# Gate/up weights of a top-2-of-8 expert layer in wider blocks, a gather in two steps, and expert rows turned in banks of their own

## The reference

```python
for i in range(2):
    z = rms_norm(h) @ w_in[i]                      # 1024 x 7168
    ... short convolutions, a gated linear recurrence, three 1024 x 1024 projections, residual add
    n2 = rms_norm(h)
    h += swiglu(n2, ffn_w_gu, ffn_w_dn)            # layer 0, width 3072
    h += moe_swiglu(n2, router, moe_w_gu, moe_w_dn)  # layer 1
    h += sigmoid(rms_norm(h) @ w_ple_gate[i]) * (p[i] @ w_ple_proj[i])

def moe_swiglu(x, router, w_gu, w_dn):   # top 2 of 8, softmax over the two logits
    for e in range(8):                   # w_gu[e] 1024 x 3072 (gate | up), w_dn[e] 1536 x 1024
        g, u = split(x @ w_gu[e])
        out += comb[:, e] * ((silu(g) * u) @ w_dn[e])
```

## Time and profile before

| | |
|---|---|
| profiled execution | 1185.72 us, span 1184.0 us |
| TensorE matmuls busy | 1126.7 us, 95% of the span |
| TensorE weight loads busy | 996.1 us, 84% |
| VectorE busy | 948.7 us, 80% |
| ScalarE busy | 721.0 us, 61% |
| moved by DMA | 289.55 MB, mean 245 GB/s |
| of it instructions, queue q8 | 92 packets, 1.51 MB |
| mean granted TensorE clock | 0.986 of full speed |
| costliest group | L1367 on VectorE, 179 of 2287 ns on the raw buffers |
| gate/up matmuls L879, L881, L882 | 1536 each, starts some 0.04 us apart |

### The profile page before, as it was taken

How to read it: one execution, slowest core, us unless ns; L and a number is a source line. 1 busy time by engine, 2 the same in 40 slices (tenths; PEclk the granted TensorE clock), 3 DMA queues, 4 the chain that set the end, 5 groups by cost and what they waited for, 6 DMA issues and landing times.

```text
span 1184.0 us, 31432 instructions
## 1 busy us (share of the span) xinstructions
PE 1126.7 (95%) x13839; PEld 996.1 (84%) x13839; DVE 948.7 (80%) x1011; ACT 721.0 (61%) x716; POOL 24.9 (2%) x59
## 2 busy tenths in 40 slices
PE   7999999999999999899999998899989998989997
PEld 4888888878888888688888885788989988988976
DVE  5986896786666657996788678499899899899877
ACT  4555744446555445445574436687888787688653
POOL 4000001000000001000000100000000000000000
PEclk7999999999999999999999999899999999999999
DMA  9665566645656563456565665699999999999911
GB/s 268 219 211 182 178 213 196 200 143 183 202 184 210 182 212 125 142 167 213 191 205 190 205 201 195 233 367 390 394 392 393 392 393 393 380 393 393 366 50 37
DMA packets 195672, 289.55 MB, mean 245 GB/s; under 512 B 5208, under 2 KB 132200, under 8 KB 195543
## 3 DMA queue, kind: packets, MB, share of 16 engines
q1 hardware_dynamic: 193830, 283.71, 68.8%
q0 software_dynamic: 1728, 4.16, 1.3%
HBM read 286.53 MB, written 1.52 MB: 243 GB/s over the span
## 4 chain that ended last, share of the span: by engine, by line
PE 78%; DVE 16%; ACT 3%; issue 2%; DMA 0%; SPq 0%; DVEq 0%; ACTq 0%
PE acc L600 16%; PE acc L602 16%; PE acc L601 16%; DVE wl L1367 10%; PE acc L879 4%; PE acc L881 3%; PE acc L882 3%; PE acc L914 2%; PE acc L585 2%; PE acc L592 2%; PE acc L586 2%; PE acc L931 2%; PE acc L934 2%; PE acc L933 2%; PE aux L832 2%
## 5 line engine op out<-in xcount | busy, mean ns | idle before, releaser
L1367 DVE SCALAR_TENSOR_TENSOR wl<-raw,wh 128x2048 f16<-128x2048 f32 x179 | 408.6, 2287 | 116.1 <-ACT wh L1012 115.4
L600 PE MATMUL acc<-xn,wh 128*128 128x264 f16 x1424 | 393.0, 276 | 0.6 <-DVE wl L1367 0.6
L602 PE MATMUL acc<-xn,wl 128*128 128x264 f16 x1424 | 393.0, 276 | 0.0
L601 PE MATMUL acc<-xn,wh 128*128 128x264 f16 x1424 | 393.0, 276 | 0.0
L1012 ACT ACTIVATE wh<-raw 128x2048 f16<-128x2048 f32 x179 | 340.2, 1907 | 7.7 <-PE acc L934 3.2
L879 PE MATMUL acc<-ga,wh 128*128 128x96 f16 x1536 | 204.3, 207 | 8.2 <-issue 4.7
L881 PE MATMUL acc<-ga,wh 128*128 128x96 f16 x1536 | 204.0, 207 | 3.9 <-issue 3.8
L882 PE MATMUL acc<-ga,wl 128*128 128x96 f16 x1536 | 204.0, 207 | 3.7 <-issue 3.7
L879 PEld LDWEIGHTS acc<-ga,wh 128*128 128x128 f16 x1536 | 151.3, 98 | 12.1 <-issue 11.5
L600 PEld LDWEIGHTS acc<-xn,wh 128*128 128x128 f16 x1424 | 139.3, 98 | 21.9 <-ACT wh L1012 0.8
L601 PEld LDWEIGHTS acc<-xn,wh 128*128 128x128 f16 x1424 | 139.3, 98 | 21.0
(11 more groups left out here) (304 smaller groups left out, 1861.7 us busy)
## 6 DMA issues: line engine op xcount, KB each, us to landing
raw<-in_w_in SPq DMA_DIRECT2D x56, 1024.0 KB, 5.1
raw<-in_moe_w_gu SPq DMA_DIRECT2D x38, 1024.0 KB, 13.0
raw<-in_ffn_w_gu SPq DMA_DIRECT2D x24, 1024.0 KB, 5.2
raw<-in_moe_w_dn SPq DMA_DIRECT2D x22, 1024.0 KB, 15.1
raw<-in_ffn_w_dn SPq DMA_DIRECT2D x12, 1024.0 KB, 5.1
ya<-in_moe_w_gu SPq DMA_DIRECT2D x11, 1024.0 KB, 14.1
xn<-in_moe_w_gu SPq DMA_DIRECT2D x11, 1024.0 KB, 13.8
xb<-in_moe_w_gu SPq DMA_DIRECT2D x10, 1024.0 KB, 14.4
```

What stands on the lines that cost most here:

```text
L600: nc.tensor.matmul(bank, hi, x[:, 0, x0 + k, :], start=(k == 0), stop=False)
L601: nc.tensor.matmul(bank, hi, x[:, 1, x0 + k, :], start=False, stop=False)
L602: last = nc.tensor.matmul(bank, lo, x[:, 0, x0 + k, :], start=False, stop=(k == k_chunks - 1))
L1367: op(V.scalar_tensor_tensor(out=wl[:, s, 0:size], in0=raw_slot[raw_turn(n)[0]][:, 0:size], scalar=WS, in1=wh[:, s, 0:size], op0=ALU.mult, ...
```

## The change

Gate/up units become 2 chunks by 1024 columns. Four units make a block of 1024 columns: gate columns 0 to 1023, then gate 1024 to 1535 with up 0 to 511, then up 512 to 1535. Both acc banks 0 and 1 are filled by one block and evacuated together after its fourth unit. Each step has two gate/up units. The gather of the next expert is done in two halves, after steps 0 and 1. The transposes of an expert's rows go to aux banks 2 and 3 (acc 0 and 1 for the last expert), and all experts keep acc banks 2 and 3 for the down projection.

```diff
-GU_K, DN_K = C // 2, 2
+GU_K, DN_K = 2, 2
+BLOCK = C // GU_K
 def gate_up_units(t):
-    return range(0 if t == 0 else 2 * t + 1, min(2 * t + 3, MOE_GU))
+    return range(2 * t, 2 * t + 2)
 # SP
-                            k, col = u % 2 * GU_K, u // 2 % 2 * FE + u // 4 * 512
-                            moe_load(gu_unit(i, u), gu[:, i, k:k + GU_K, col:col + 512], GU_K)
+                            k, col = u % BLOCK * GU_K, u // BLOCK * 1024
+                            moe_load(gu_unit(i, u), gu[:, i, k:k + GU_K, col:col + 1024], GU_K)
 # TensorE
+        def rows_bank(e, half):
+            return acc[0:CAP, half, :] if e == NE - 1 else aux[0:CAP, 2 + half, :]
-            def gather(e):
-                for g in range(4):
+            def gather(e, groups):
+                for g in groups:
...
+                    if e > 2 and g > 1:
+                        pe.wait_ge(ys_ready, 2 * (e - 3) + g - 1)
 # gate_or_up
+                for m in range(C):
+                    bank = acc[:, m // 4, m % 4 * CAP:(m % 4 + 1) * CAP]
+                    if s == 0 and m % 4 == 0:
+                        if block == 0 and e:
+                            pe.wait_ge(up_out, GROUPS * (e - 1) + m // 4 + 2)
+                        elif block == 1:
+                            pe.wait_ge(gate_out, GROUPS * e + m // 4 + 1)
+                        elif block == 2:
+                            pe.wait_ge(*((gate_out, GROUPS * e + 3) if m == 0 else (up_out, GROUPS * e + 1)))
             def slots_to_rows(e):
+                if e < NE - 1:
+                    pe.wait_ge(gat_done, 4 * min(e + 2, NE - 1) + 4)
+                    if e:
+                        pe.wait_ge(sc_done, 8 * e)
 # down
-                if d == 0 and e == NE - 1:
-                    pe.wait_ge(gate_out, GROUPS * NE)
-                    pe.wait_ge(up_out, GROUPS * NE)
-                elif d == 0 and e:
-                    pe.wait_ge(ys_ready, 2 * e)
+                if d == 0 and e:
+                    pe.wait_ge(down_out, 2 * e)
 # TensorE's loop
                     if i + 1 < NE and t == 0:
                         pe.wait_ge(sel_ready, i + 2)
-                        gather(i + 1)
+                        gather(i + 1, (0, 1))
                     if i + 1 < NE and t == 1:
+                        gather(i + 1, (2, 3))
                         selected_slots(i + 1)
 # ScalarE, after the router's Exp
+            nc.scalar.activation(root[:], eps[:], ACT.Silu)
 # ScalarE, gate_or_up
-                if u % 4 == 1 and q:
+                if u == 1 and e:
+                    hidden_hi(q - 2)
                     hidden_hi(q - 1)
+                if u == 9:
+                    hidden_hi(q)
+                if u % BLOCK == BLOCK - 1:
+                    act.wait_ge(unit_mm, n + 1)
+                    if u == BLOCK - 1:
+                        if e:
+                            act.wait_ge(hid_w, q)
+                        gate(0)
+                        gate(1)
+                    elif u == 2 * BLOCK - 1:
+                        gate(2)
+                        up(0)
+                    else:
+                        up(1)
+                        act.wait_ge(hid_w, q + 1)
+                        up(2)
 # ScalarE and VectorE, the loops
-                            if i > 1 and u == 0:
+                            if i > 1 and u == 1:
                                 expert_out(i - 2)
 # VectorE, gate_or_up
+                if u == 2 * BLOCK - 1:
+                    product(0)
+                if u == MOE_GU - 1:
+                    product(1)
+                    product(2)
-                    if i + 1 < NE and t == 2:
+                    if i + 1 < NE and t == 3:
                         slot_weights(i + 1)
```

More of the change, by code:

```diff
@@ L119, in gu_unit @@
 def gu_unit(e, u):
-    return moe_base(e) + u + (max(u - 1, 0) // 2 if e else 0)
+    return moe_base(e) + u + (u // 2 if e else 0)
 def dn_unit(e, d):
@@ L852, in scatter @@
                         pe.wait_ge(selt_ready, min(e + 4, NE))
-                    pe.wait_ge(ys_ready, 2 * e + c // 4 + 1)
+                    pe.wait_ge(ys_ready, 2 * e + (2 if c > 2 else 1))
                     if c < 4 and e + 3 >= NE and e:
@@ L861, in gate_or_up @@
             def gate_or_up(e, u):
[L863 to L868, removed]
+                n, s, block = gu_unit(e, u), u % BLOCK, u // BLOCK
+                if block == 0:
+                    pe.wait_ge(gat_done, 4 * e + s + 1)
                 pe.wait_ge(hi_done, TURN[n] + 1)
@@ L877, in gate_or_up @@
                         x_hi, x_lo = (xg[:, e % 2, i, s * GU_K + k, :] for i in range(2))
-                        end = s == 1 and k == GU_K - 1
-                        nc.tensor.matmul(bank, hi, x_hi, start=(s == 0 and m == 0 and k == 0), stop=False,
+                        end = s == BLOCK - 1 and k == GU_K - 1
+                        nc.tensor.matmul(bank, hi, x_hi, start=(s == 0 and m % 4 == 0 and k == 0), stop=False,
                                          skip_group_check=True)
@@ L893, in slots_to_rows @@
                         at = (4 * half + m) * CAP
-                        last = nc.tensor.transpose(acc[0:CAP, ye_bank(e) + half, m * P:(m + 1) * P], yt[:, at:at + CAP],
+                        last = nc.tensor.transpose(rows_bank(e, half)[:, m * P:(m + 1) * P], yt[:, at:at + CAP],
                                                    ident[:])
@@ L939, in _ @@
             pe.wait_ge(sel_ready, 1)
-            gather(0)
+            gather(0, range(4))
             selected_slots(0)
@@ L959, in _ @@
                         scatter(i - 2, range(2 * t - 4, 2 * t))
+            pe.wait_ge(up_out, GROUPS * NE)
             slots_to_rows(NE - 1)
@@ L1244, in _, with gathered @@
                 act.nop()
-            def gathered(e):
-                for g in range(4):
+            def gathered(e, groups):
+                for g in groups:
                     act.wait_ge(gat_full, 4 * e + g + 1)
@@ L1878, in gate_or_up, with product @@
             def gate_or_up(e, u):
-                n, q = gu_unit(e, u), GROUPS * e + u // 4
+                n, q = gu_unit(e, u), GROUPS * e
                 if n > N_MOE:
                     lo(ahead(n))
-                if u % 4 == 1 and q:
+                if u == 1 and e:
+                    hidden_lo(q - 2)
                     hidden_lo(q - 1)
-                if u % 4 == 3:
-                    b = q % 2
-                    vec_e.wait_ge(gate_out, q + 1)
-                    vec_e.wait_ge(up_out, q + 1)
-                    split = is_split(q)
-                    op(V.scalar_tensor_tensor(out=moe_w[:, b, :] if split else hid_32[:, e % 2, :], in0=moe_g[:, b, :],
+                if u == 9:
+                    hidden_lo(q)
+                def product(g):
+                    b, split = (q + g) % 2, is_split(q + g)
+                    vec_e.wait_ge(gate_out, q + g + 1)
+                    vec_e.wait_ge(up_out, q + g + 1)
+                    vec_e.wait_ge(hid_ready, count[hid_ready])
+                    op(V.scalar_tensor_tensor(out=moe_w[:, b, :] if split else hid_32[:, e % 2, :], in0=moe_g[:, g, :],
                                               scalar=XS if split else XS * WS, in1=moe_u[:, b, :],
                                               op0=ALU.mult, op1=ALU.mult), hid_w)
+                if u == 2 * BLOCK - 1:
[3 more added lines that the diff above has]
+                    product(2)
             def down(e, d):
@@ L1903, in expert_out @@
                     vec_e.wait_ge(ye_hi, 2 * e + half + 1)
-                    op(V.scalar_tensor_tensor(out=ye[0:CAP, 1, s], in0=acc[0:CAP, ye_bank(e) + half, :],
+                    op(V.scalar_tensor_tensor(out=ye[0:CAP, 1, s], in0=rows_bank(e, half),
                                               scalar=csl[0:CAP, e % 4:e % 4 + 1], in1=ye[0:CAP, 0, s],
```

44 lines of the change are left out of this document (19 added, 25 removed).

## The result

The changed kernel takes 1191.64 us (median of 6 runs, 1190.27 to 1194.52), beside 1186.41 us for the kernel before in the same comparison (6 runs, 1184.89 to 1187.89). The ratio is 1.0046, with a 95% interval of 1.0031 to 1.0061: slower by 5.5 us (3.7 to 7.2). I had forecast 1187.7, with 1178.5 to 1194.5 as the range. The profiled execution ran 1190.72 us with a span of 1189.0, 5.0 above the span before.

The account below looks back on a forecast made before the run. The prediction took TensorE's pace (work plus issue) to bound the expert stage, VectorE close behind. Its terms, -4.1 + 5.6 - 1.6 + 2.4 - 0.8 + 0.5 = +2.0 us, gave 1187.7 us, range 1178.5 to 1194.5.

Parts of the forecast that it names:

- rival B: Expert stage: the wait for adds bites in full, 9.2 us, with three clock falls, 4.8 us; 1194.5 us, chance 0.23.
- signs of being wrong: Transposes' waits under 1 us or over 4, mid-stage waits for weights, or issue time changed by more than 3 us.
- Part 3: Down projection of a new expert no longer waits for the output leaving the down banks: -4.1 us, and -1.6 of clock.
- Part 4: Transposes in iterations 3, 5 and 7 newly wait for VectorE's scattered adds: +5.6 us, and +2.4 of clock.
- upper bound of 9.2: Waits of the transposes for the adds, in us, if VectorE's idle time in even iterations is kept.
- I count the idle as gone.: VectorE's idle in even iterations, 1.07, 1.66 and 1.07 us, vanishes with the two-step gather, leaving waits of 2.8, 2.2 and 0.3.
- Part 2: Gate/up matmuls: same 48 per unit in another order over two banks, issue time unchanged: 0; bounds -19.6 to +3.7 us.
- Clock: TensorE's clock falls behind waits: 1.6 us removed with the output wait, one and a half new falls add 2.4.
- Part 1: Gate/up loads in 4 KB rows: 405 instead of 387 GB/s, 11.6 us of transfers over 8 experts, hidden by TensorE: 0.
- rival C: Expert stage: loads set the pace, so the quicker loads save 11.6 us; 1174.1 us, chance 0.05.
- Part 5: Ends: early table load costs 0.8 us and removes 1.6 of VectorE's idle, net -0.8; last expert's split adds +0.5.
- The split of the second group: Last expert: one step later, its 0.5 us come ahead of what TensorE needs for the third down unit: +0.5.

Follow-up runs that it names:

- e1: Changed kernel with VectorE's second four adds of an iteration moved ahead of the conversion at unit 11, 4.5 us earlier: 1185.63 us, ratio 0.9995.
- e4: Changed kernel with the next expert's gather in one step, all four banks after step 0: 1193.52 us, ratio 1.0064.
- e5: Kernel before, with gate/up loads of 2 chunks by 1024 columns (4 KB rows) and nothing else changed: 1184.62 us, ratio 0.9986.
- e6: Changed kernel with gate/up loads of 4 chunks by 512 columns (2 KB rows) as before: 1194.78 us, ratio 1.0072.
- e9: Changed kernel with rows of experts 0 to 5 in the accumulation banks again and the expert's output back behind unit 0: 1197.69 us, ratio 1.0104.
- e12: As e9, with steps cut as before: three gate/up units ahead of an iteration's first down unit: 1191.3 us, ratio 1.0038.
- e3: Changed kernel with 14 unused matmuls of 512 columns added before each of the three transposes that wait for the adds: 1189.92 us, ratio 1.0026.
- e7: Changed kernel without the small Silu behind the Exp, so the table load is at the first Silu again: 1191.43 us, ratio 1.0040.
- e8: Kernel before, with the small Silu behind the Exp (early table load) as the only change: 1186.62 us, ratio 1.0005.
- e11: As e1, with the last expert's down projection in accumulation banks 0 and 1 and its rows in 2 and 3: 1185.91 us, ratio 0.9995.

## Why the prediction came out as it did

The sum said +2.0, the rows say +5.1 and the comparison +5.5: within the range, just outside the forecast's own 1184 to 1191, and between the forecast and rival B (+8.8). The mechanism is rival B's, to which I gave 0.23: VectorE's idle time was not recovered, and all three waits bit in full. Two of my own signs of being wrong came up: one wait is over 4 us (4.2), and "issue" changed by more than 3 (3.8). That the time fell inside the range is in part luck, since the stalls that went (-3.8) made up for most of the waits that I had priced too low (+5.5).

**Part 3 was right.** TensorE waits nowhere in the stage for the output, so -4.1. What the account left out is why such a wait is there: as I read it now, it is TensorE's lead over VectorE at the end of an even iteration. e1 shows such a wait coming back at what ties the two together next.

**Part 4 is the step that failed, by size.** The place, the mechanism and the iterations (3, 5 and 7) were right; 2.9, 2.3 and 0.4 us became 4.2, 3.5 and 3.4, 11.1 instead of 5.6 and above my upper bound of 9.2. Two assumptions failed:

- "I count the idle as gone." VectorE's idle time in the three even iterations was 3.8 us and is 3.1 after (0.91 at 858.00, 0.44, and 1.74 in three pieces), and e4 shows that the gather in two steps is not what the waits hang on. Why the idle stays is argued, not shown: ScalarE waits there for TensorE to free a slot, so it would be time in which VectorE is ahead.
- The positions of the earlier trace rows were carried over as they stood. In the rows of after, from unit 0 of an even iteration to the end of VectorE's adds it is 51.4, 50.9 and 51.8 us, and TensorE arrives 47.3, 47.5 and 48.5 us after the same start (start of the transpose less the idle before it): the wait is the difference of two paces. Before, the same two counts were 51.5, 52.1 and 51.0, and 47.5, 48.1 and 49.6. So in the three together VectorE became 0.5 us quicker and not 3.8, and TensorE 1.9: 9.4 us of waits with nothing changed, less 0.5, plus 1.9, plus 0.1 for each wait, are the 11.1. Of TensorE's 1.9 us 1.1 are in iteration 6 (1023.06 to 1072.65 us before), where it lost 4.9 us to "issue" and weights; after, 3.5. I had priced the third wait at 0.3 because of these stalls.

**Part 2 was taken as 0 and is -3.8 by the rows.** I let the issue time hang on the number of instructions alone, and weighed larger packets only as a delay for them (+3.7 at most). With the same instructions and larger packets it fell (e5), with smaller ones it rose (e6). In e5 1.7 of 3.1 us reach the time. In the changed kernel part of it goes into the wait of part 4, which is 10.2 us with rows of 2 KB (e6) and 11.1 with 4 KB. So the two errors, +5.5 and -3.8, are in part the same one.

**Part 2's other half, which I passed over:** that a step has two gate/up units instead of three at the start and one at the end. I costed it as an order of matmuls. By e9 and e12 it is +7.8 us against the steps of before if the rows stay where they were, as much as any part of the change, and it is what the banks of its own pay for.

**Clock:** I counted one and a half falls, 2.4 us, less 1.6; it is 3.4 less 1.6, in one trace. e3's 2.4 does not contradict it.

**Part 1 was right in its term:** 406 GB/s instead of 387 and no gain by the loads' own pace; e5 does not come near the 11.6 us of rival C. The gain it has comes by another way, the stalls.

**Part 5:** start -0.8; the early load alone measures +0.7 us in the changed kernel (e7 to after) and +0.6 in the kernel before (e8), neither clear of 0. Its two halves were priced about right, 0.7 lost and 1.3 gained in idle time; the gain does not show in the time. The split of the second group, +0.5: not seen as a wait. In its stead 1.0 us at the last expert's first down unit, since the last expert no longer has banks of its own for the down projection; I had not listed it, and e11 shows that it is not worth its time.

I also wrote that the waits would be put down to the adds. The profile put them down to "issue"; e3's did name them.

Put together from the comparisons (each step with some 2.5 us of uncertainty): packets -1.7 (e5), blocks of four on the old steps, with all that comes with them, +6.2 (e5 to e12; the 8.7 us of evacuations stand against shorter stalls), two units to a step +7.8 (e12 to e9), banks of their own -6.9 (e9 to the changed kernel): +5.4. The parts act on one another, so in another order the same steps would be worth something else.

## What to carry to other kernels

Where two engines take turns at being the slower one, price a wait as the difference of their paces from the point where they last met, not from the positions that the trace happens to show; a gain for the faster engine can then go into the wait. Idle time of the engine that does the late work is no reserve by itself: it has to be shown what it waits for. And when a tiling changes, look first at what stands between each producer and its consumer in the new order: one unit less between rows and down projection cost 7.8 us here (e12 to e9), and I had put it at nothing.

## What the hardware showed that I had not expected

- With 4 KB rows instead of 2 KB rows, TensorE's "issue" time in a stage that DMA keeps full fell from 19.6 to 16.5 us (e5) and rose from 15.8 to 19.8 us the other way (e6), with the same instructions in the same order. Every one of these stalls ends 1.2 to 1.6 us behind the end of a packet of the instruction queue.
- A long wait hides instruction stalls: with the three waits removed, "issue" went from 15.8 to 19.4 us (e1). Of the difference 2.2 us are two stalls that end at 981.88 and 988.17 us in e1, right behind the place of the second wait, where the changed kernel has none.
- Three waits of TensorE of 3.4 to 4.2 us brought the clock to 0.51 behind two of them. With 3.21 us of matmuls in the gap and 0.81 us left of the wait (e3) it stayed at 1.00. In e9 waits of 3.8 to 4.5 us were followed by half speed each time. Which of the three waits is followed by a fall changes with little: the first and second in the changed kernel, the first and third in e7, all three in e6.
